# Second attention of a two-block model on one core: maximum inside the sum, another order of steps, outputs split in place

## The chip, the cores and the metric

One core of a Trainium2 chip runs the whole program. The time is device microseconds of one execution, and the number given is the median of the runs. The engines are PE (matmuls), DVE and ACT (vector and scalar work), POOL and SP (here the queue of the weight loads). Each has its own queue of instructions and executes it in order; engines meet in semaphores only.

## The reference, cut to what matters

Two model blocks follow each other on one sequence of 512 tokens of width 1024, in float32. The change touches the last layer of the second block alone, a differential attention with 8 heads of two score maps each:

```python
def diff_attention_layer(x, k, v, norm_g, w_in, lam_qk, sub_g, w_out, lambda_init):
    qg = rms_norm_2(x, norm_g) @ w_in
    q, gate = qg[..., :1024], qg[..., 1024:]        # q: 4 blocks of 128 tokens, 8 heads, 2 maps, 64
    lam = jnp.exp(jnp.sum(lf[0] * lf[1])) - jnp.exp(jnp.sum(lf[2] * lf[3])) + lambda_init
    slopes = 2.0 ** -jnp.arange(1, 9)
    def attend_block(args):
        scores = jnp.einsum("bhiqd,bhikd->bhiqk", qb, k) / math.sqrt(64)
        scores = scores - slopes[None, :, None, None, None] * dist
        probs = jax.nn.softmax(jnp.where(allowed, scores, -jnp.inf), axis=-1)
        weights = probs[:, :, 0] - lam * probs[:, :, 1]
        return jnp.einsum("bhqk,bhke->bqhe", weights, v)
    out = rms_norm_2(out, sub_g) * (1.0 - lambda_init)
    return x + (out * jax.nn.silu(gate)) @ w_out
```

`dist` is the distance of query and key, `allowed` holds for keys whose chunk of 64 is not later than the query's. A final RMS norm follows.

## The kernel before, in words

All matrices lie transposed in SBUF, eight tiles of 128 rows by 512 tokens. A dense product keeps float32 precision with three matmuls for each tile of 128 by 128: the weight and the activation are both split into a high part (type fp32r) and the rest (`xh`, `xl`; `wh`, `wl`), and high by high, high by low and low by high are added in PSUM (`product`, L387). A dense tile is so 8 x 3 = 24 matmuls of 512 columns.

Weights come in one long list of units (`weight_units`, L211), whose sequence is that of the program; the host packs them in that sequence. SP loads unit n into one of five buffers (L339), ACT writes the high half into one of three (`split_hi`, L351), DVE subtracts to get the low half (`split_lo`, L362). ACT and DVE work LA = 2 units ahead of PE, and wait for PE to be done with the unit three earlier.

The program has six stages: an S5 layer, a feed-forward, an attention, a feed-forward, a Mamba-2 layer and the second attention. Each engine walks through each stage with its own function (`att2_pe`, `att2_act`, `att2_dve`, `att2_pool`, from L2452). In the second attention all four walk over the same hand-made list of steps, `att2_order()` (L167), and each issues what its engine has in that step. The order of this list is therefore each engine's order of work.

The steps of the list, with the block number n = 4 x head + query block, or with the head or the tile m:

- `query m`, `gate m` (each one dense tile of `b_w_in_2`) and `out m` (tiles of `b_w_out_2`, first half: heads 0 to 3 only). ACT and DVE split the unit LA ahead in the same step. `queryB` (DVE, L2535) scales the query's result from PSUM, `gateB` multiplies the gate's with the norm (DVE, L2539) and takes its tanh (ACT, L2498), `gateC` finishes the gate (DVE, L2542), `outB` adds to h (L592).
- `scores n`: PE multiplies queries and keys of both maps (L2321), 128, 256, 384 or 512 key columns for query block 0 to 3, into four PSUM banks in turn.
- `exps n`: DVE adds the distances, times the slope, to each map (L2333), then reduces the maxima of both (L2337); ACT takes the exponential with the maximum as its bias and the sum as a second output (L2346).
- `combine n`: DVE inverts the sums, multiplies with lambda and forms the weights (L2355 to L2359).
- `turn n`: PE transposes the weights into one PSUM bank (L2367); `keep n`: ACT copies them out (L2375). The next `turn` needs that copy.
- `mix hd`: when the four blocks of a head are kept, PE multiplies them with the values (L2384). `sumsq hd`: ACT copies the result (L2393) and squares it (L2396), PE sums the squares over the head's 128 rows (L2402). `rs hd`: DVE forms the variance (L2408), ACT takes Ln and Exp for the inverse root (L2414, L2416; another table than the one of tanh). `tail hd`: DVE makes one Newton step in three instructions (L2422 to L2425), multiplies with the norm (L2428) and with the gate (L2431). `split hd`: DVE copies the high part into `xh` (L2437), POOL subtracts for the low part into `xl` (L2443).

The `xh` and `xl` tiles hold the attention's input until the last gate tile is done, so `split` waits for that (XUSED[10]), and the list places the splits there. After the list come the second halves of the eight output tiles, which need heads 4 to 7, then the sum of squares, the final norm (L2563) and the stores.

```python
        for r in list(running):
            out.append(r.pop(0))
        if 0 <= n - 4 < 32:
            out.append(("keep", n - 4))
            if (n - 4) % 4 == 3:
                running.append([("mix", hd), ("sumsq", hd), ("rs", hd), ("tail", hd)])
        if dense and n % 2 == 0:
            out.append(dense.pop(0))
```

In short (the full text is printed below), a slot n of the old list first takes one step of every running sequence, then `keep n-4`, `exps n-1`, `combine n-2`, `scores n`, every second slot a dense tile, and `turn n-3`. The first `out` comes in slot 31.

## Time and profile before

| what | value |
|---|---|
| runs, us | 2274.14, 2279.8, 2276.79; median 2276.79 |
| profiled execution, us | 2273.84 |
| its span, us | 2272.0 |
| granted TensorE clock over the span | 0.949 of full speed |
| second attention, from its first scores | 2012 us to the end |

The profiled execution's own time is 2273.84 us, 1.84 us more than its span; the span is what every view of the trace is counted in. Busy times of an engine are sums over its instructions; PE's are taken at the clock that was granted, so a slow stretch looks busier than a fast one. The idle time in front of an instruction is put down to what released it last.

### The profile page before, as it was taken

What the parts mean: (1) busy time and instruction counts of PE and PEld (TensorE: products, weight loads), DVE (VectorE), ACT (ScalarE), POOL (GpSimd) and SP (SyncE); (2) the same over time, 40 slices, a digit from 0 to 9 for tenths busy, and PEclk for the clock granted to TensorE, in tenths of its full rate; (3) what the DMA queues carried; (4) which work ended last, traced back from release to release, by engine and by line L of the source; (5) the groups of instructions that cost most, each with busy time, mean ns of one, the idle gap of its engine ahead of it and who ended that gap; (6) DMA issues with size and microseconds to landing.
All of it is one profiled execution on the core that took longest, in us unless ns stands there. A gap on an engine that the chain in (4) does not pass through costs nothing.

```text
span 2272.0 us, 24722 instructions
## 1 busy us (share of the span) xinstructions
PE 2036.6 (90%) x9332; PEld 1596.9 (70%) x9332; DVE 1450.1 (64%) x2058; ACT 829.2 (36%) x1246; POOL 227.1 (10%) x179
## 2 busy tenths in 40 slices
PE   5786899999999987799999998889999988998876
PEld 3575778888887855677888886667777767865545
DVE  7895457536644457647636645678787776257775
ACT  3334333222233335433322234344434334245542
POOL 2000010000010000010000010232222322000012
PEclk9887999999999989999999999899999999998888
DMA  5253423232232210022233222112222213321001
GB/s 194 71 132 81 133 74 103 83 111 95 81 112 94 83 57 1 1 85 93 83 111 97 84 91 83 46 52 65 70 64 66 71 46 100 108 67 42 19 28 60
DMA packets 86646, 178.32 MB, mean 78 GB/s; under 512 B 25856, under 2 KB 39296, under 8 KB 86528
## 3 DMA queue, kind: packets, MB, share of 16 engines
q1 hardware_dynamic: 84864, 171.56, 24.6%
q0 software_dynamic: 1376, 4.13, 0.6%
q8 instruction: 75, 1.23, 0.2%
q10 hardware_dynamic: 288, 1.05, 0.1%
q14 instruction: 43, 0.35, 0.0%
HBM read 169.43 MB, written 7.27 MB: 78 GB/s over the span
## 4 chain that ended last, share of the span: by engine, by line
PE 71%; DVE 15%; ACT 7%; issue 5%; DMA 1%; SPq 1%; POOL 0%; DVEq 0%; POOLq 0%; ACTq 0%
PE psum L398 18%; PE psum L401 17%; PE psum L399 17%; DVE wl L369 2%; PE psum L416 2%; PE psum L417 2%; PE psum L419 2%; ACT wh L358 1%; PE psum L761 1%; PE psum L763 1%; PE psum L762 1%; PE psum L1552 1%; PE psum L947 1%; PE psum L2384 1%; ACT ww L964 1%
## 5 line engine op out<-in xcount | busy, mean ns | idle before, releaser
L369 DVE TENSOR_TENSOR wl<-raw,wh 128x1024 fp32r<-128x1024 f32 (+3 forms) x337 | 385.4, 1144 | 433.4 <-ACT wh L358 432.9
L398 PE MATMUL psum<-xh,wh 128*128 128x512 f32 x1544 | 625.5, 405 | 20.9 <-DVE h L592 14.8
L401 PE MATMUL psum<-xh,wl 128*128 128x512 f32 x1544 | 610.3, 395 | 1.3 <-DVE wl L369 1.3
L399 PE MATMUL psum<-xl,wh 128*128 128x512 f32 x1544 | 609.8, 395 | 0.0
L358 ACT ACTIVATE wh<-raw 128x1024 fp32r<-128x1024 f32 (+3 forms) x337 | 314.9, 937 | 316.9 <-PE psum L401 214.3
L398 PEld LDWEIGHTS psum<-xh,wh 128*128 128x128 f32 x1544 | 295.6, 191 | 99.3 <-issue 17.5
L401 PEld LDWEIGHTS psum<-xh,wl 128*128 128x128 f32 x1544 | 294.9, 191 | 66.1 <-DVE wl L369 3.2
L399 PEld LDWEIGHTS psum<-xl,wh 128*128 128x128 f32 x1544 | 295.6, 191 | 65.0 <-issue 4.6
L515 POOL TENSOR_TENSOR rs<-rs,sq 128x512 f32<-128x512 f32 x49 | 67.1, 1369 | 1165.8 <-ACT sq L500 1164.9
L398 PE MATMUL psum<-fh,wh 128*128 128x512 f32 x352 | 139.2, 396 | 0.0
L401 PE MATMUL psum<-fh,wl 128*128 128x512 f32 x352 | 139.2, 396 | 0.0
L399 PE MATMUL psum<-fl,wh 128*128 128x512 f32 x352 | 139.2, 395 | 0.0
L592 DVE TENSOR_TENSOR h<-h,psum 128x512 f32<-128x512 f32 x88 | 60.2, 684 | 86.8 <-PE psum L401 85.7
L416 PE MATMUL psum<-xh,wh 128*128 128x512 f32 x184 | 77.3, 420 | 34.4 <-ACT wh L358 15.9
L401 PEld LDWEIGHTS psum<-fh,wl 128*128 128x128 f32 x352 | 66.1, 188 | 16.1
L399 PEld LDWEIGHTS psum<-fl,wh 128*128 128x128 f32 x352 | 66.1, 188 | 16.0
L398 PEld LDWEIGHTS psum<-fh,wh 128*128 128x128 f32 x352 | 66.1, 188 | 15.9
L419 PE MATMUL psum<-xh,wl 128*128 128x512 f32 x184 | 75.0, 408 | 1.4 <-DVE wl L369 1.4
L417 PE MATMUL psum<-xl,wh 128*128 128x512 f32 x184 | 75.1, 408 | 0.0
L480 ACT ACTIVATE xh<-h,par 128x512 fp32r<-128x512 f32 x64 | 44.0, 716 | 71.8 <-DVE h L592 56.6
L416 PEld LDWEIGHTS psum<-xh,wh 128*128 128x128 f32 x184 | 36.7, 200 | 45.3 <-issue 26.3
L398 PE MATMUL psum<-muh,wh 128*128 128x512 f32 x128 | 55.0, 429 | 8.7 <-POOL mul L1626 5.5
(430 smaller groups left out, 2994.4 us busy)
## 6 DMA issues: line engine op xcount, KB each, us to landing
raw<-d_w SPq DMA_DIRECT2D x224, 512.0 KB, 3.5
raw<-d_w SPq DMA_DIRECT2D x32, 384.0 KB, 3.0
raw<-d_w SPq DMA_DIRECT2D x48, 256.0 KB, 2.7
raw<-d_w SPq DMA_DIRECT2D x32, 320.0 KB, 2.9
Mt<-d_kd SPq DMA_DIRECT2D x64, 64.0 KB, 2.4
bc<-d_bc SPq DMA_DIRECT2D x8, 256.0 KB, 4.1
d_ud<-ust SPq DMA_DIRECT2D x8, 256.0 KB, 3.6
U<-d_ud SPq DMA_DIRECT2D x64, 32.0 KB, 2.1
```

Source lines behind the costliest of these rows:

```text
L358: act.e.activation(K.wh[n % NH][:, 0:COLS[n]], K.raw[n % RAW][:, 0:COLS[n]], ACT.Copy).then_inc(K.S["hi"], 1)
L369: dve.e.tensor_tensor(K.wl[n % NH][:, 0:COLS[n]], K.raw[n % RAW][:, 0:COLS[n]], K.wh[n % NH][:, 0:COLS[n]].bitcast(F32), ALU.subtract).the ...
L398: pe.e.matmul(b[:, :], WH[:, o:o + P], XH, start=(k == k0), stop=False)
L399: pe.e.matmul(b[:, :], WH[:, o:o + P], XL, start=False, stop=False)
L401: mm = pe.e.matmul(b[:, :], WL[:, o:o + P], XH, start=False, stop=(k == k1 - 1))
L416: pe.e.matmul(b[:, :], WH[:, o:o + P], XH, start=(k == 0), stop=False)
L417: pe.e.matmul(b[:, :], WH[:, o:o + P], XL, start=False, stop=False)
L419: mm = pe.e.matmul(b[:, :], WL[:, o:o + P], XH, start=False, stop=(k == 7))
L480: act.e.activation(K.xh[:, k, :], K.h[:, k, :], ACT.Copy, scale=K.par(gain, k)).then_inc(K.S["xh"], 1)
L515: pool.e.tensor_tensor(K.acc[:, :], K.acc[:, :], K.sq[k % 2][:, :], ALU.add).then_inc(K.S["acc"], 1)
L592: dve.e.tensor_tensor(K.h[:, m, :], K.h[:, m, :], K.bank[bank][:, :], ALU.add).then_inc(K.S[signal], 1)
L761: pe.e.matmul(b[:, :], XH[:, c], WH[:, kk * 512:(kk + 1) * 512], start=(k == 0), stop=False)
```

## The change

What it does, in the order of the diff:

- The list of steps is written anew. A slot n now holds, in this order: the steps put first (`queryB` and `gateB` one slot after their dense tile, `gateT` (the tanh, ACT) two after, `gateC` three after, `square` (the copy and the square of a mixed head, ACT), `outB`), `scores n`, a dense tile where one is due, `turn n-3`, `exps n-1`, `combine n-2`, `keep n-3`, and the steps put last. The 14 dense tiles stand in slots 0, 2, 5, 7, 10, 12, 14, 17, 19, 21, 24, 26, 29 and 31, the eight first output halves in slots 33 to 40. A head's end, from one slot after its fourth `keep`, takes one slot each for `mix`, `sumsq`, `rs`, `tailA` (the Newton step), `tailB` (the two products) and `split`, all as the slot's last steps, with `square` first in the slot of `sumsq`.
- Sum and maximum are one DVE instruction for each map. It adds scores and distances, multiplies by -2^-(hd+1), stores, and gives the minimum out into the bias. The query's scale holds 2^(hd+1) in return, and the exponential is taken with scale -1.
- The high part of a finished head goes by ACT into a tile `oh` of its own, the low part by POOL into `ol`. `oh` lies where the keys `kT2` lie and `ol` where the queries `qT2` lie, so the low part is written over the value it is made from; the high part waits until the head's scores are done (`asp`). The waits for the last gate tile are gone. The output product reads `oh` and `ol`.

```diff
--- before.py
+++ after.py
@@ -166,43 +166,42 @@
 def att2_order():
-    out = [("query", 0), ("queryB", 0), ("query", 1)]
-    running = [[("queryB", 1)]]
     dense = [x for m in range(8) for x in ([("query", m + 2)] if m < 6 else []) + [("gate", m)]]
-    outs, splits, n = list(range(8)), 0, 0
-    while n < 36 or running or splits < 8:
-        for r in list(running):
-            out.append(r.pop(0))
-            if not r:
-                running.remove(r)
-        if not dense and splits < 8 and ("tail", splits) in out:
-            out.append(("split", splits))
-            splits += 1
-        if 0 <= n - 4 < 32:
-            out.append(("keep", n - 4))
-            if (n - 4) % 4 == 3:
-                hd = (n - 4) // 4
-                running.append([("mix", hd), ("sumsq", hd), ("rs", hd), ("tail", hd)])
+    at = {(k * 31 + 6) // 13: x for k, x in enumerate(dense)}
+    assert len(at) == 14 and max(at) < 33
+    out = [("query", 0), ("queryB", 0), ("query", 1), ("queryB", 1)]
+    later = {}
+    for n in range(41):
+        out += later.get((n, "first"), [])
+        if n < 32:
+            out.append(("scores", n))
+        if n in at:
+            what, m = at[n]
+            out.append((what, m))
+            later.setdefault((n + 1, "first"), []).append((what + "B", m))
+            if what == "gate":
+                later.setdefault((n + 2, "first"), []).append(("gateT", m))
+                later.setdefault((n + 3, "first"), []).append(("gateC", m))
+        if 33 <= n:
+            out.append(("out", n - 33))
+            later.setdefault((n + 1, "first"), []).append(("outB", n - 33))
+        if 0 <= n - 3 < 32:
+            out.append(("turn", n - 3))
         if 0 <= n - 1 < 32:
             out.append(("exps", n - 1))
         if 0 <= n - 2 < 32:
             out.append(("combine", n - 2))
-        if n < 32:
-            out.append(("scores", n))
-        if dense and n % 2 == 0:
-            what, m = dense.pop(0)
-            out.append((what, m))
-            running.append([(what + c, m) for c in ("B", "C")] if what == "gate" else [(what + "B", m)])
-        if n >= 31 and outs:
-            m = outs.pop(0)
-            out.append(("out", m))
-            running.append([("outB", m)])
         if 0 <= n - 3 < 32:
-            out.append(("turn", n - 3))
-        n += 1
-    for m in outs:
-        out += [("out", m), ("outB", m)]
-    return out
+            out.append(("keep", n - 3))
+            if (n - 3) % 4 == 3:
+                hd = (n - 3) // 4
+                for k, what in enumerate(("mix", "sumsq", "rs", "tailA", "tailB", "split")):
+                    later.setdefault((n + 1 + k, "last"), []).append((what, hd))
+                later.setdefault((n + 2, "first"), []).append(("square", hd))
+        out += later.get((n, "last"), [])
+    return out + [("outB", 7)]
 S5_ORDER, MAMBA_ORDER, ATT2_ORDER = s5_order(), mamba_order(), att2_order()
@@ -2330,20 +2329,19 @@
     dve.wait_ge("ld", 16)
     for c in range(2):
         dve.wait_ge("asp", 2 * n + c + 1)
-        dve.e.scalar_tensor_tensor(out=S[:, c, 0:nk], in0=K.con("alibi")[:, T - nk:T], scalar=2.0 ** -(hd + 1),
-                                   in1=K.bank[2 + (2 * n + c) % 4][:, 0:nk], op0=ALU.mult, op1=ALU.add).then_inc(
-            K.S["asc"], 1)
-    dve.wait_ge("asc", 2 * n + 2)
-    dve.e.tensor_reduce(sv[:, 0:2], S[:, :, 0:nk], AX.X, ALU.max, negate=True).then_inc(K.S["amx"], 1)
+        last = dve.e.tensor_tensor_reduce(S[:, c, 0:nk], K.bank[2 + (2 * n + c) % 4][:, 0:nk],
+                                          K.con("alibi")[:, T - nk:T], -(2.0 ** -(hd + 1)), 3e38, ALU.add, ALU.min,
+                                          sv[:, c:c + 1])
+        last.then_inc(K.S["asc"], 1)
 def exps_act(K, act, n):
     nk = P * (n % 4 + 1)
     S, sv = K.Sb[n % 2], K.sml[:, n % 16, :]
-    act.wait_ge("amx", n + 1)
+    act.wait_ge("asc", 2 * n + 2)
     act.exp()
     for c in range(2):
-        act.e.activation(S[:, c, 0:nk], S[:, c, 0:nk], ACT.Exp, bias=sv[:, c:c + 1],
+        act.e.activation(S[:, c, 0:nk], S[:, c, 0:nk], ACT.Exp, scale=-1.0, bias=sv[:, c:c + 1],
                          accum_out=sv[:, 2 + c:3 + c]).then_inc(K.S["aex"], 1)
@@ -2416,14 +2414,19 @@
     act.e.activation(K.ny[:, :], K.ny[:, :], ACT.Exp, scale=-0.5).then_inc(K.S["any"], 1)
-def tail2_dve(K, dve, hd):
-    o, s, y, e = K.qT2[:, hd, :], K.ns, K.ny, dve.e
+def newton2_dve(K, dve, hd):
+    s, y, e = K.ns, K.ny, dve.e
     dve.wait_ge("any", hd + 1)
     own(K, dve, "dve", e.scalar_tensor_tensor(out=s[:, :], in0=y[:, :], scalar=-0.5, in1=y[:, :], op0=ALU.mult,
                                               op1=ALU.mult))
     own(K, dve, "dve", e.tensor_tensor(s[:, :], s[:, :], K.nv[:, :], ALU.mult))
-    own(K, dve, "dve", e.scalar_tensor_tensor(out=y[:, :], in0=s[:, :], scalar=1.5, in1=y[:, :], op0=ALU.add,
-                                              op1=ALU.mult))
+    e.scalar_tensor_tensor(out=y[:, :], in0=s[:, :], scalar=1.5, in1=y[:, :], op0=ALU.add,
+                           op1=ALU.mult).then_inc(K.S["dve"], dve.up())
+def tail2_dve(K, dve, hd):
+    o, y, e = K.qT2[:, hd, :], K.ny, dve.e
+    dve.wait_ge("dve", dve.n)
     dve.wait_ge("asq", hd + 1)
     own(K, dve, "dve", e.scalar_tensor_tensor(out=o, in0=o, scalar=K.lam[:, 6:7], in1=y[:, :], op0=ALU.mult,
                                               op1=ALU.mult))
@@ -2431,17 +2434,26 @@
     e.tensor_tensor(o, o, K.gS[hd % 4][:, :], ALU.mult).then_inc(K.S["aot"], 1)
-def split2_dve(K, dve, hd):
-    dve.wait_ge("aot", hd + 1)
-    dve.wait_ge("unit", XUSED[10])
-    dve.e.tensor_copy(K.xh[:, hd, :], K.qT2[:, hd, :]).then_inc(K.S["xh"], 1)
+def split2_act(K, act, hd):
+    act.wait_ge("aot", hd + 1)
+    act.wait_ge("asp", 8 * hd + 8)
+    act.e.activation(K.oh[:, hd, :], K.qT2[:, hd, :], ACT.Copy).then_inc(K.S["xh"], 1)
 def split2_pool(K, pool, hd):
     pool.wait_ge("xh", 88 + hd + 1)
-    pool.wait_ge("unit", XUSED[10])
-    pool.e.tensor_tensor(K.xl[:, hd, :], K.qT2[:, hd, :], K.xh[:, hd, :].bitcast(F32), ALU.subtract).then_inc(
+    pool.e.tensor_tensor(K.ol[:, hd, :], K.qT2[:, hd, :], K.oh[:, hd, :].bitcast(F32), ALU.subtract).then_inc(
         K.S["xl"], 1)
+def out2_x(K, pe):
+    def x(k):
+        pe.wait_ge("xh", 88 + k + 1)
+        pe.wait_ge("xl", 88 + k + 1)
+        return K.oh[:, k, :], K.ol[:, k, :]
+    return x
 def tile2(what, m):
@@ -2457,7 +2469,7 @@
     values_pe(K, pe, "w_kv_2", x, 8)
     x = x_of(K, pe, 10)
     product_pair(K, pe, "b_w_in_2", (0, 1), (0, 1), x, (("aqc", 1), ("aqc", 2)))
-    xo = x_of(K, pe, 11)
+    xo = out2_x(K, pe)
     for what, m in ATT2_ORDER:
         if what == "query" and m > 1:
             product(K, pe, "b_w_in_2", m, B2[(what, m)], x, ("aqc", m + 1))
@@ -2491,7 +2503,7 @@
     for what, m in ATT2_ORDER:
         if what in ("query", "gate", "out"):
             split_hi(K, act, done(*tile2(what, m)) + LA)
-        elif what == "gateB":
+        elif what == "gateT":
             act.wait_ge("agg", m + 1)
             act.wait_ge("agt", m - 1)
             act.other("tanh")
@@ -2500,8 +2512,10 @@
             keep2_act(K, act, m)
         elif what == "exps":
             exps_act(K, act, m)
-        elif what == "sumsq":
+        elif what == "square":
             sumsq_act(K, act, m)
+        elif what == "split":
+            split2_act(K, act, m)
         elif what == "rs":
             rs2_act(K, act, m)
     for m in range(8):
@@ -2532,7 +2546,7 @@
             split_lo(K, dve, done(*tile2(what, m)) + LA)
         elif what == "queryB":
             dve.wait_ge("unit", done(*tile2("query", m)))
-            dve.e.scalar_tensor_tensor(out=K.qT2[:, m, :], in0=K.bank[B2[("query", m)]][:, :], scalar=0.125,
+            dve.e.scalar_tensor_tensor(out=K.qT2[:, m, :], in0=K.bank[B2[("query", m)]][:, :], scalar=0.125 * 2.0 ** (m + 1),
                                        in1=K.rs[:, :], op0=ALU.mult, op1=ALU.mult).then_inc(K.S["aqc"], 1)
         elif what == "gateB":
             dve.wait_ge("aot", m - 3)
@@ -2549,10 +2563,10 @@
             combine2_dve(K, dve, m)
         elif what == "rs":
             rs2_dve(K, dve, m)
-        elif what == "tail":
+        elif what == "tailA":
+            newton2_dve(K, dve, m)
+        elif what == "tailB":
             tail2_dve(K, dve, m)
-        elif what == "split":
-            split2_dve(K, dve, m)
     for m in range(8):
         v = done("b_w_out_2", m, 4, 8)
         split_lo(K, dve, v + LA)
@@ -2736,9 +2750,13 @@
                     mamba_tensors(K, sb)
                 else:
                     att2_tensors(K, sb)
-                    K.kT2 = sb("k2T", [P, 8, T])
-                    K.qT2 = sb("q2T", [P, 8, T])
                     K.Vt["w_kv_2"] = sb("V2t", [P, 4, D])
+                    with ExitStack() as inner:
+                        sb = lambda name, shape, dt=F32: inner.enter_context(nc.sbuf_tensor(name, shape, dt))
+                        K.kT2, K.qT2 = sb("k2T", [P, 8, T]), sb("q2T", [P, 8, T])
+                    sb = lambda name, shape, dt=F32: part.enter_context(nc.sbuf_tensor(name, shape, dt))
+                    K.oh, K.ol = sb("oh", [P, 8, T], R32), sb("ol", [P, 8, T], R32)
         block = ctx.enter_context(nc.Block())
```

## Rows read from the trace of the kernel before

**Rows 1.** The page's first lines: span, and busy us, share, instructions of each engine
```profile
span 2272.0 us, 24722 instructions
...
PE 2036.6 (90%) x9332; PEld 1596.9 (70%) x9332; DVE 1450.1 (64%) x2058; ACT 829.2 (36%) x1246; POOL 227.1 (10%) x179
```

**Rows 2.** Busy time by stretch (count), granted clock, DMA share, GB/s
```profile
2012.00:2191.00 179.00, 147.70 (x595) 97.92 (x595) 135.88 (x282) 90.41 (x205) 5.14 (x4) 0.90 0.11 34
2191.00:2233.00 42.00, 34.05 (x137) 25.48 (x135) 30.70 (x54) 14.33 (x29) 5.78 (x4) 0.92 0.16 51
...
2255.00:2272.00 17.00, 2.07 (x2) 0.50 (x2) 8.79 (x13) 1.89 (x3) 1.75 (x2) 0.56 0.32 123
```

**Rows 3.** Same view, four heads of the loop: the first and the mean
```profile
2060.00:2086.00 26.00, 21.05 (x86) 14.15 (x85) 19.45 (x40) 13.56 (x29) 0.00 (x0) 0.87 0.13 41
...
sum 104.00, PE 83.75 PEld 56.17 DVE 77.28 ACT 54.30 POOL 0.00; mean PE 20.94 PEld 14.04 DVE 19.32 ACT 13.57 POOL 0.00
```

**Rows 4.** Waits, 2012 to 2233: engine, line, releaser, us in total, times, longest
```profile
ACT S L2346 <- DVE small L2337: 51.9, 24, 8.7
...
PE psum L2367 <- ACT wT L2375: 26.0, 8, 5.1
DVE wl L369 <- ACT wh L358: 22.5, 16, 2.6
```

**Rows 5.** Chain of waits, around one head's mix and at the end: start, us, what
```profile
2112.21 0.70 DVE nv L2408
2112.92 1.28 ACT L2685
2114.21 0.64 ACT ny L2414
...
2123.90 0.49 ACT wT L2375
...
2133.80 0.23 PE psum L398
...
2134.70 0.86 PE psum L2402 x2
...
2234.03 0.43 PE psum L399
```

**Rows 6.** Timeline of PE: start, us, engine, line, operation, idle before
```profile
2012.25 0.49 PE L2321 MATMUL psum<-k2T,q2T 64*128 64x128 f32 x4 [2.39 <-DVE q2T L2535]
...
2124.71 3.68 PE L2384 MATMUL psum<-wT,V2t 128*128 128x512 f32 x8
...
2190.99 0.50 PE L398 MATMUL psum<-xh,wh 128*128 128x512 f32 x1
...
2216.74 2.32 PE L2384 MATMUL psum<-wT,V2t 128*128 128x512 f32 x8
...
2233.27 0.77 PE L398 MATMUL psum<-xh,wh 128*128 128x512 f32 x1 [3.06 <-POOL xl L2443]
```

**Rows 7.** DVE groups by form, 2012 to 2255: count, busy us, mean ns, idle
```profile
L2333 DVE SCALAR_TENSOR_TENSOR S<-con,psum 128x512 f32<-128x512 f32 x16 | 10.2, 681 | 0.0
...
L2359 DVE SCALAR_TENSOR_TENSOR w<-S,small,w 128x512 f32<-128x512 f32 x8 | 6.0, 751 | 0.3
...
L2333 DVE SCALAR_TENSOR_TENSOR S<-con,psum 128x128 f32<-128x128 f32 x16 | 3.8, 279 | 0.0
...
L2359 DVE SCALAR_TENSOR_TENSOR w<-S,small,w 128x128 f32<-128x128 f32 x8 | 2.8, 351 | 0.3
```

**Rows 8.** Groups by line, 1900 to 2272
```profile
L2337 DVE TENSOR_REDUCE small<-S 128x2 f32<-128x256 f32 (+3 forms) x32 | 26.2, 820 | 1.1
...
L2346 ACT ACTIVATION_READ_ACCUMULATOR S<-S,small 128x1 f32 x64 | 12.0, 187 | 0.0
...
L2393 ACT ACTIVATE q2T<-psum 128x512 f32<-128x512 f32 x8 | 4.6, 577 | 1.5 <-PE psum L2384 1.5
L2437 DVE CAST xh<-q2T 128x512 fp32r<-128x512 f32 x8 | 3.4, 420 | 0.0
```

## The prediction

> **What bounds the kernel now.** The page's totals come first: PE is busy for 2036.6 of 2272.0 us, DVE for 1450.1 [rows 1]. That is an average over six stages, and the diff touches only the last, so the second view is the busy time by stretch. The loop over 32 score blocks runs from 2012 us to 2191 us, the eight first halves of the output product come among the last heads' work until about 2230, then the second halves until 2255, then the final norm and the stores (17 us) [rows 2]. In the first stretch PE is busy for 147.70 of 179 us and DVE for 135.88: neither is full. PE's figure is also flattered: the granted clock is 0.90, and four middle stretches of 26 us, one head each, repeat themselves with 20.9 us of PE, 19.3 of DVE and 13.6 of ACT in the mean, the first at a clock of 0.87 [rows 3]. Since no engine fills a head's 26 us, waits set the pace.
>
> The waits by engine say which [rows 4]. PE idles 26.0 us in 8 waits, up to 5.1 us each, for the copy of the turned weights (L2375); DVE idles 22.5 us for a high half of a weight (L358); ACT idles 51.9 us for the maxima (L2337). The chain of waits shows why these belong together [rows 5]. Once a head it runs in series: variance (L2408), a load of ACT's table 1.28, Ln, Exp, an earlier block's exponentials, a weight's high half, its low half on DVE, Newton steps, two products for the tail, the gate on DVE, its tanh, and only then the copy (0.49) that lets PE turn the next block and mix. From 2112.21 to 2124.4 PE is on none of it; it runs a dense product and the scores and then idles, and the mix behind takes 3.68 us at 2124.71, the same eight matmuls that take 2.32 at 2216.74 [rows 6]: the clock had fallen to the lower level after the idle stretch. The end has a second knot: at 2233.27 PE has waited 3.06 us for POOL's low half of head 7 [rows 6], and its following matmuls run 0.43 us apart where others of that form run 0.23 apart [rows 5].
>
> **The maximum in the sum.** 32 reductions (L2337) leave DVE, 820 ns each, 26.2 us [rows 8]. The 64 sums (L2333: 681 ns at 512 columns, 279 at 128 [rows 7]) become 64 instructions that add, scale, store and keep a minimum. The trace of before has none of that kind. Lower bound: nothing beyond the sum it replaces. Nearest row for a maximum or sum given out beside the stream: ACT's read of its accumulator, 187 ns [rows 8]; it overlaps the next exponential, and about half of it delays that one, so I take 0.10 us, 6.4 us in all. Upper bound: half the rate. Between 128 and 512 columns the sum rises by (681-279)/384 = 1.05 ns a column; 64 instructions over 20480 columns would then cost 21.4 us more.
> The two source streams and the reduced result invite one rule of the Trainium skill (Vector Engine (DVE) Microarchitecture Reference, "Points that are easy to get wrong"): a scalar-tensor-tensor with two sources in SBUF that are not bf16 halves its throughput, with no port left for the accumulator. The trace doesn't bear this out for f32: L2359 reads two SBUF tensors and takes 751 ns at 512 columns against 351 at 128, again 1.04 ns a column [rows 7]. [...]
> The scale of 2^(hd+1) goes into the query's factor and the sign into the exponential's scale: no instruction more, nothing. DVE so loses 26.2 - 6.4 = 19.8 us, of which what counts is about 2.5 us a head before the exponentials.
>
> **The splits of the outputs.** Eight casts of 420 ns leave DVE [rows 8]: 3.4 us. ACT gets eight copies of 128x512, 0.58 us by L2393 [rows 8]: 4.6 us on an engine that is busy 13.6 of 26. POOL's subtractions stay. The added wait for the scores of the head is met long before, since the head's mix follows them. Queued behind the ACT copy are the next exponentials; 0.6 us there is hidden by the slot of lag that DVE's combination has. Because results go to their own place, heads 0 to 6 are split as they come, none in a batch after the last gate.
>
> **The new order.** Both orders hold 14 dense tiles of 24 matmuls; the spacing goes from 2 slots (score blocks) to 31/13 = 2.38, so the first output half stands at slot 33, not 31. Table loads stay at 12 by the order of tanh and Ln. The gate is now three steps (product with rs, tanh, product), the norm's Newton steps and its last two products sit a slot apart, and each slot of DVE puts the maxima before the combination of the block ahead. SP loads the units in their new sequence; it runs up to five buffers ahead and DMA's share is 0.11 in the loop [rows 2], so nothing. No wait is on POOL before head 0's split.
>
> I walked four slots (one head) of the new lists by hand. Work: DVE 19.3 in rows 3, less 3.3 of reductions, plus 0.8, 16.8 us; PE, mix at full clock, about 18.0 with two dense tiles. What is left of waiting on DVE: some 1.1 us for a dense product to end before its result is taken, 0.9 for Ln and Exp behind the table load (1.28, 0.64, 0.64 [rows 5]), and 2 for a high half that stands behind a tanh and its load. Together 20.8 us, 5.2 a slot, where rows 3 have 6.5. No PE gap in it is over 2 us, so I leave the clock at its upper level. The first ten slots have four dense products (24 x 0.23 = 5.5 us each) but hardly norms or tails: the same walk gives 37.4 us. So the first output half starts 37.4 + 23 x 5.2 = 157 us after 2012.25, where it now starts 2190.99 - 2012.25 = 178.7 after [rows 6]: 21.7 less.
>
> **The end.** From the first output half to the second halves PE has 8 x 12 matmuls at 0.23, 22 us, mix 7 (2.1, by its 2.32 [rows 6] less the overlap with the next), two sums of squares (0.86 each [rows 5]) and two turns (0.8): 26.5 us. Now it takes 37.2 (2190.99 to about 2228.2, that is 2233.27 less 3.06 and less nine matmuls): 10.7 less. The tail of head 7 (rs, Ln, Exp, Newton, products, copy, low half) needs some 11 us and has outputs 3 to 7 before it, 13.7 us: the wait of 3.06 goes, and the eight matmuls at the lower clock behind it (8 x 0.2): 4.7 less. If that cover fails, these 4.7 come back. The second halves, the final norm and the stores (2255 to 2272 [rows 2]) stay.
> Sum: 21.7 + 10.7 + 4.7 = 37.1; I take off 1 for hand-overs that a walk doesn't count: 36. The profiled execution was 2273.84 (span 2272.0), 2.95 below the median of the runs, so this is 2237.8 for such an execution and 2241 against the median 2276.79. About 0.3% (7 us) is what a measurement here can tell from no change.
>
> **Rivals.**
> A. The new instruction runs at half rate, since its result needs a port beside the two streams: 21.4 us where I took 6.4, 15.0 more on DVE, plus what a later maximum costs ACT; DVE is then nearly full, so I count it whole: 2257. For it: a reduction and a two-source stream in one; against: L2359's slope. Chance 0.10. [...]
> B. The in-order queues keep a serial chain. ACT's copy of turned weights waits behind a dense product on PE, and Ln, Exp, tanh and the high half queue behind it; if this costs half of the 1.3 us a slot that I take away, 23 x 0.65 = 15 us return: 2256. For it: rows 5. Against: tail and gate no longer share a slot. Chance 0.13.
> C. The overlap is better and PE is the bound: 18.0 us a head where I have 20.8 gives 0.7 a slot, 16 us: 2225. For it: PE's work. Against: it allows no waiting. Chance 0.13.
> D. Slower. DVE has to change programs between its built-in operations and the added one, as ACT does with its tables (1.28 us, rows 5). Once a slot on DVE, the engine every slot passes: 32 x 1.28 = 41 us, 5 more than I gain: 2282. It decides from 36/32 = 1.1 us a slot. Against: no such change shows on DVE anywhere. Chance 0.03.
> My forecast keeps 0.61.
>
> **How the numbers follow.** 2241 is the likeliest. Its own spread is some 8 us; C reaches down to 2225, A and B to 2257 with their own spread. The range 2224 to 2260 leaves out most of D, and the outer parts of A, B and C, about 0.15. Faster by over 0.3%: all cases but D and a small part of B, 0.94; within 0.3%: 0.03; slower: 0.03.
>
> **What would show it.** No reduction, and 64 new instructions near 780 ns at 512 columns and 380 at 128; PE's wait for L2375 near a quarter of 26 us; a clock above 0.95 in the loop; score blocks 20.8 us a head; PE's first output half near 2169; no wait of PE for POOL at the end. A new instruction near 1.2 us at 512 columns means A; a wait of 3 us or more of PE once a head means B; DVE gaps before or behind each new pair mean D.

## The result and the profile after

The changed kernel takes **2252.02 us** (median of 4 runs, 2248.75 to 2258.05) where the kernel before takes 2278.3 (4 runs, 2274.14 to 2285.96): ratio 0.9884, interval 0.9849 to 0.9919, so 26 us less, 18 to 34 by the interval. A second measurement (e0 below) gave 0.9893 (0.9862 to 0.9924). The forecast was 36 less, 2241, with the range 2224 to 2260: direction and range hold, the size was 10 us too large.

First the totals of the page after, against [rows 1]:

```profile
span 2248.4 us, 24757 instructions
...
PE 2036.6 (91%) x9332; PEld 1596.5 (71%) x9332; DVE 1424.4 (63%) x2082; ACT 833.6 (37%) x1254; POOL 226.3 (10%) x179
```

Over the whole program PE's busy time is the same and the span 23.6 us less; DVE's busy time is 25.7 us less, ACT's 4.4 more. Where the gain lies is best read between five marks that both kernels have: the first scores, the scores of head 2's third block (slot 10), those of head 6's third block (slot 26), the first output half, and the last addition to h. The ten slots ahead of slot 10 are called the ramp below. Busy time by stretch, after; columns as in [rows 2]:

```profile
2016.00:2056.60 40.60, 38.45 (x162) 26.20 (x162) 24.65 (x78) 17.89 (x47) 0.00 (x0) 0.96 0.20 65
2056.60:2140.30 83.70, 75.79 (x313) 50.04 (x312) 64.90 (x170) 53.03 (x120) 4.71 (x4) 0.96 0.11 32
2140.30:2179.70 39.40, 33.40 (x133) 21.94 (x133) 27.43 (x71) 23.29 (x49) 1.69 (x2) 0.91 0.07 21
2179.70:2232.20 52.50, 50.55 (x211) 39.47 (x209) 34.41 (x55) 22.06 (x39) 11.52 (x9) 0.97 0.17 46
```

The same view of the kernel before, between the same marks:

```profile
2012.30:2058.80 46.50, 43.52 (x186) 30.60 (x186) 33.34 (x71) 19.53 (x50) 0.00 (x0) 0.96 0.19 61
2058.80:2162.90 104.10, 83.85 (x337) 56.23 (x336) 77.38 (x157) 54.22 (x118) 0.00 (x0) 0.89 0.10 29
2162.90:2191.00 28.10, 20.28 (x74) 11.04 (x73) 24.86 (x55) 16.66 (x39) 5.14 (x4) 0.82 0.03 10
2191.00:2255.00 64.00, 55.63 (x224) 42.95 (x222) 41.35 (x67) 21.36 (x41) 13.14 (x10) 0.92 0.12 38
```

The reader sees four things. The ramp is 6.1 us shorter, but it also holds one dense tile less (162 matmuls for 186, 5.1 us less of PE's work), because the new list spaces them more widely. Sixteen middle slots take 83.7 us instead of 104.1: PE is busy for 8.1 us less (24 matmuls fewer lie in it, and the clock is 0.96 instead of 0.89), and its idle time falls from 20.3 to 7.9. The last slots are 11.3 us *longer*, because 59 more matmuls, 13.1 us of PE's work, now lie in them and not ahead of them. The output products take 52.5 instead of 64.0, with 13 matmuls fewer in them, and PE is idle for 2.0 of them instead of 8.4. From the last addition to the end it is 16.2 against 17.05. Summed over these stretches PE's busy time falls by 6 us, the same matmuls at a higher granted clock, and its waiting by some 21. So from the first scores to the end the profiled executions take 232.3 against 259.8: 27.5 less. The first scores themselves stand at 2016.1 against 2012.25, 3.9 later, ahead of everything that was changed. Over all kernels of this study that mark lies anywhere from 2010.9 to 2024.6 us, with the same instructions in front of it. Therefore the experiments are compared by **the stretch from the first scores to the end**, and by medians where there are several runs. In e0 the stretch repeated as 232.3, though there the first scores stood in the same place too (2016.2). For another place only parts can be compared: in e7 the first scores stand 8 us later, and the ramp, the same list of steps there, takes 40.55 us against 40.50.

The waits after, 2012 to 2225, against [rows 4]:

```profile
ACT S L2344 <- DVE small L2332: 54.2, 22, 8.3
DVE wl L368 <- ACT wh L357: 43.2, 21, 5.5
...
PE psum L2400 <- ACT sq L2394: 6.1, 5, 2.7
...
PE psum L2365 <- ACT wT L2373: 5.9, 7, 1.7
```

PE's wait for the copy of turned weights fell from 26.0 us to 5.9. But DVE's wait for a weight's high half rose from 22.5 to 43.2, and the one for the squares, 8.6 us in 2 places before, is 6.1 in 5 (L2400). Each half of the change raises it by itself: it is 37.5 us in e1 below, which keeps the old order, and 36.1 (2020 to 2240) in e2, which keeps the old maximum. What the wait holds up is a matter of the order on DVE. Timeline of DVE in one head after (start, us, engine, line, operation, idle before):

```profile
2095.76 0.62 DVE L2357 SCALAR_TENSOR_TENSOR w<-S,small,w 128x384 f32<-128x384 f32 x1
2098.32 1.48 DVE L368 TENSOR_TENSOR wl<-raw,wh 128x1024 fp32r<-128x1024 f32 x1 [1.94 <-ACT wh L357]
2099.72 0.28 DVE L2332 CUSTOM_DVE_ANT_0 S<-psum,con 128x128 f32<-128x128 f32 x1
...
2106.49 0.69 DVE L2423 SCALAR_TENSOR_TENSOR ny<-xs,ny 128x512 f32<-128x512 f32 x1
2109.40 1.22 DVE L368 TENSOR_TENSOR wl<-raw,wh 128x1024 fp32r<-128x1024 f32 x1 [2.22 <-ACT wh L357]
2110.55 0.55 DVE L2332 CUSTOM_DVE_ANT_0 S<-psum,con 128x384 f32<-128x384 f32 x1
```

and ACT beside it:

```profile
2102.43 1.28 ACT L2699 ACT_TABLE_LOAD   x1
2103.72 0.63 ACT L2412 ACTIVATE ny<-nv 128x512 f32<-128x512 f32 x1
2104.38 0.63 ACT L2414 ACTIVATE ny<-ny 128x512 f32<-128x512 f32 x1
...
2105.90 0.58 ACT L2373 ACTIVATE wT<-psum 128x512 f32<-128x512 f32 x1
2106.50 1.28 ACT L2510 ACT_TABLE_LOAD   x1
2107.79 0.63 ACT L2510 ACTIVATE gt<-gate 128x512 f32<-128x512 f32 x1
2108.33 1.04 ACT L357 ACTIVATE wh<-raw 128x1024 fp32r<-128x1024 f32 x1
```

DVE stands 2.22 us for the high half (L357), which ACT makes only behind a table load and a tanh. Behind DVE's low half (L368) stand the maxima of the next block (L2332), whose scores PE has long finished and whose exponentials ACT needs next. Work that is due several slots later holds up work that is due now. The chain of waits of the kernel after goes round just that way:

```profile
2102.43 1.28 ACT L2699
2103.72 0.64 ACT ny L2412
...
2104.92 1.08 ACT S L2344 x4
2106.00 0.48 ACT wT L2373
2106.50 1.28 ACT L2510
2107.79 0.63 ACT gt L2510
2108.43 0.96 ACT wh L357
...
2109.40 0.04 DVE wl L368
...
2110.55 0.55 DVE S L2332
```

The new instruction, DVE's groups by form, 2016 to 2231, against [rows 7]:

```profile
L2332 DVE CUSTOM_DVE_ANT_0 S<-psum,con 128x512 f32<-128x512 f32 x16 | 10.4, 684 | 0.0
...
L2332 DVE DVE_READ_ACCUMULATOR2_ANT small<- 128x1 f32 x64 | 5.2, 82 | 0.0
...
L2332 DVE CUSTOM_DVE_ANT_0 S<-psum,con 128x128 f32<-128x128 f32 x16 | 3.9, 282 | 0.0
```

It takes 684 ns at 512 columns and 282 at 128, where the sum took 681 and 279: (684 - 282)/384 = 1.05 ns a column, the same slope. The result is handed out by a second instruction of 82 ns, which starts with the next one and lies beside it.

### The profile page after: what moved, and what is told of

Its sections match the earlier page's. It is cut to its first block, busy times and chain, and to the rows that moved or that the text cites. A ratio compares the mean times of both kernels' runs of the same rounds, so it can differ in the third digit from the quotient of the medians.

```text
span 2248.4 us, 24757 instructions
## 1 busy us (share of the span) xinstructions
PE 2036.6 (91%) x9332; PEld 1596.5 (71%) x9332; DVE 1424.4 (63%) x2082; ACT 833.6 (37%) x1254; POOL 226.3 (10%) x179
## 3 DMA queue, kind: packets, MB, share of 16 engines
q10 hardware_dynamic: 288, 1.05, 0.2%
## 4 chain that ended last, share of the span: by engine, by line
PE 70%; DVE 15%; ACT 7%; issue 5%; DMA 1%; SPq 1%; POOL 0%; DVEq 0%; POOLq 0%; ACTq 0%
PE psum L397 18%; PE psum L400 18%; PE psum L398 18%; PE psum L415 2%; PE psum L418 2%; PE psum L416 2%; DVE wl L368 2%; ACT wh L357 1%; PE psum L760 1%; PE psum L761 1%; PE psum L762 1%; PE psum L1551 1%; PE psum L946 1%; DVE S L2332 1%; ACT ww L963 1%
## 5 line engine op out<-in xcount | busy, mean ns | idle before, releaser
L368 DVE TENSOR_TENSOR wl<-raw,wh 128x1024 fp32r<-128x1024 f32 (+3 forms) x337 | 386.2, 1146 | 448.1 <-ACT wh L357 447.5
L397 PE MATMUL psum<-xh,wh 128*128 128x512 f32 x1480 | 596.8, 403 | 17.1 <-DVE h L591 14.9
L400 PE MATMUL psum<-xh,wl 128*128 128x512 f32 x1480 | 583.4, 394 | 1.3 <-DVE wl L368 1.3
L398 PE MATMUL psum<-xl,wh 128*128 128x512 f32 x1480 | 583.4, 394 | 0.0
L357 ACT ACTIVATE wh<-raw 128x1024 fp32r<-128x1024 f32 (+3 forms) x337 | 314.9, 937 | 320.6 <-PE psum L400 214.9
L397 PEld LDWEIGHTS psum<-xh,wh 128*128 128x128 f32 x1480 | 282.6, 191 | 93.3 <-DVE h L591 16.1
L400 PEld LDWEIGHTS psum<-xh,wl 128*128 128x128 f32 x1480 | 282.2, 191 | 63.4 <-DVE wl L368 3.2
L398 PEld LDWEIGHTS psum<-xl,wh 128*128 128x128 f32 x1480 | 282.5, 191 | 62.0 <-issue 3.9
L415 PE MATMUL psum<-xh,wh 128*128 128x512 f32 x184 | 79.9, 434 | 34.0 <-ACT wh L357 15.9
L418 PE MATMUL psum<-xh,wl 128*128 128x512 f32 x184 | 77.9, 424 | 2.5 <-DVE wl L368 2.5
L416 PE MATMUL psum<-xl,wh 128*128 128x512 f32 x184 | 77.5, 421 | 0.0
L400 PEld LDWEIGHTS psum<-fh,wl 128*128 128x128 f32 x352 | 66.0, 187 | 16.2
L415 PEld LDWEIGHTS psum<-xh,wh 128*128 128x128 f32 x184 | 38.3, 208 | 45.4 <-issue 26.0
```

What stands on the lines that cost most here:

```text
L357: act.e.activation(K.wh[n % NH][:, 0:COLS[n]], K.raw[n % RAW][:, 0:COLS[n]], ACT.Copy).then_inc(K.S["hi"], 1)
L368: dve.e.tensor_tensor(K.wl[n % NH][:, 0:COLS[n]], K.raw[n % RAW][:, 0:COLS[n]], K.wh[n % NH][:, 0:COLS[n]].bitcast(F32), ALU.subtract).the ...
L397: pe.e.matmul(b[:, :], WH[:, o:o + P], XH, start=(k == k0), stop=False)
L398: pe.e.matmul(b[:, :], WH[:, o:o + P], XL, start=False, stop=False)
L400: mm = pe.e.matmul(b[:, :], WL[:, o:o + P], XH, start=False, stop=(k == k1 - 1))
L415: pe.e.matmul(b[:, :], WH[:, o:o + P], XH, start=(k == 0), stop=False)
```

## The experiments

The theory ahead of them: the two halves of the change (maximum in the sum; order and splits) each bring part of the gain, and what is missing is lost on DVE's in-order queue behind the high half. The rivals: the maximum alone brings it all; the loss is in table loads, in the new instruction, or in PE itself.

**e1, the maximum alone**, in the kernel before:

```
-        dve.e.scalar_tensor_tensor(out=S[:, c, 0:nk], in0=K.con("alibi")[:, T - nk:T], scalar=2.0 ** -(hd + 1),
-                                   in1=K.bank[2 + (2 * n + c) % 4][:, 0:nk], op0=ALU.mult, op1=ALU.add).then_inc(
...
-    dve.e.tensor_reduce(sv[:, 0:2], S[:, :, 0:nk], AX.X, ALU.max, negate=True).then_inc(K.S["amx"], 1)
+        last = dve.e.tensor_tensor_reduce(S[:, c, 0:nk], K.bank[2 + (2 * n + c) % 4][:, 0:nk],
+                                          K.con("alibi")[:, T - nk:T], -(2.0 ** -(hd + 1)), 3e38, ALU.add, ALU.min,
+                                          sv[:, c:c + 1])
...
-            dve.e.scalar_tensor_tensor(out=K.qT2[:, m, :], in0=K.bank[B2[("query", m)]][:, :], scalar=0.125,
+            dve.e.scalar_tensor_tensor(out=K.qT2[:, m, :], in0=K.bank[B2[("query", m)]][:, :], scalar=0.125 * 2.0 ** (m + 1),
```

> The kernel before with the maximum taken in the sum alone; order and splits as before. Theory (the order carries the gain): the once-a-head chain of the old order (variance, table load, Ln, Exp, high half, low half, Newton, tail, gate, tanh, copy) holds no maximum, so the middle heads keep about 26 us each and only the slots at the start and at the end get shorter: 5 to 9 us less than before, ratio about 0.997. Rival (DVE's work carries the gain): 32 slots x 0.65 us = 21 us less, ratio about 0.991, and the middle heads at about 23 us. Both expect 64 new instructions as long as the sums they replace, and 64 reads of the accumulator of 82 ns.

Measured: 2263.29, ratio 0.9947 (0.9927 to 0.9967), 12 us less; the stretch is 246.4, 13.4 less. That is above the theory's 5 to 9 and below the rival's 21; the middle heads take 25.5 us, close to the theory's 26. The waits, 2012 to 2240:

```profile
DVE wl L369 <- ACT wh L358: 37.5, 22, 5.5
...
PE psum L2366 <- ACT wT L2374: 23.9, 7, 4.7
```

PE still waits 23.9 us for the turned weights: the old serial chain stays, and it is shorter only by what DVE spends less in it. A slot between 10 and 26 takes 6.38 us, before 6.51.

**e2, all but the maximum**: the changed kernel with the sum and the reduction of before (the diff of e1 turned round, in the new order).

> The changed kernel with the old sum and reduction; its order and its splits in place stay. Theory (the order carries the gain): 12 to 18 us less than before, ratio about 0.993, heads at about 22 to 23 us. Rival (DVE's work carries it): within 5 us of before.

Measured: 2261.32, ratio 0.9936 (0.9913 to 0.9959); the stretch is 246.7, 13.1 less (its profiled execution alone, 2273.15, would mislead: the first scores stand 12 us later in it than in before). That is within the expected 12 to 18; a middle head takes 23.5 us, a little over the expected 22 to 23. e1 and e2 add to 26.5 of the 27.5 us, but by stretch the parts aren't independent. In the old order the maximum takes 8.5 us off the time up to the first output half and 5.0 off the output halves (before against e1); in the new order it takes off 14.1 and 0.4 (e2 against after). In the slots the two help each other; in the output halves the new order leaves the maximum almost nothing to gain.

**e3, only the splits** in the kernel before: ACT makes the high halves of the outputs into a place of their own, as they come.

```
-                running.append([("mix", hd), ("sumsq", hd), ("rs", hd), ("tail", hd)])
+                running.append([("mix", hd), ("sumsq", hd), ("rs", hd), ("tail", hd), ("split", hd)])
...
-    dve.e.tensor_copy(K.xh[:, hd, :], K.qT2[:, hd, :]).then_inc(K.S["xh"], 1)
+    act.e.activation(K.oh[:, hd, :], K.qT2[:, hd, :], ACT.Copy).then_inc(K.S["xh"], 1)
```

> The kernel before with the splits of the finished heads in place, by ACT, one step after each head's tail; the old order otherwise, the old maximum. Theory: 3.4 us of copies leave DVE, but in the middle heads an ACT copy of 0.6 us is added to a chain that ACT is part of, and the wait of PE for head 7 at the end stays: within 4 us of before. Rival (the waits of the splits for the last gate tile cost time): 5 to 10 us less.

Measured: ratio 0.9982 (0.9965 to 0.9999), 2272.93; the stretch 255.1, 4.7 less, all of it at the end. That is just over the theory's 4 and under the rival's 5, and the interval of the runs holds both, but the slots keep their 6.51 us. At the end PE still waits:

```profile
2228.96 0.47 PE L395 MATMUL psum<-oh,wh 128*128 128x512 f32 x1 [2.37 <-POOL ol L2441]
```

So in e2 and after it is the new place of head 7's tail, not the split alone, that takes this wait away; and the rest of e2's gain, 13.1 less these 4.7, about 8 us if the parts add, is the order. Most of it shows in the output halves (58.9 in e3, 52.9 in e2), where the new order also has 13 matmuls fewer.

**e4, the low halves behind the maxima.** The weights' low half is taken after the block's combination; the rest is the changed kernel.

```
     for what, m in ATT2_ORDER:
-        if what in ("query", "gate", "out"):
+        if what == "out":
             split_lo(K, dve, done(*tile2(what, m)) + LA)
+        elif what in ("query", "gate"):
+            late = done(*tile2(what, m)) + LA
...
             combine2_dve(K, dve, m)
+            split_lo(K, dve, late)
```

> The changed kernel with DVE's low half of a query or gate weight made after the slot's combination of the weights instead of in front of its maxima. In the changed kernel DVE waits 24.6 us in 12 of these for ACT's high half, with the maxima and the combination queued behind. Theory (that in-order wait is what keeps a head at 20.3 us where PE's own work is 18): 6 to 12 us less than the changed kernel, about 2243 against its 2252, heads at 19 us. Rival (ACT's queue itself is late, the wait only shows it): within 3 us of the changed kernel.

Measured: 2244.88, ratio 0.985 (0.9826 to 0.9873); the stretch is 222.8, 9.5 less than after, within the expected 6 to 12. The medians differ by 7 to 9 us; the intervals of the two ratios overlap, so it is the stretch that carries this reading. No instruction was added or taken away. Busy time by stretch between the marks of above, from slot 10 on, and the waits, 2018 to 2231:

```profile
2062.41:2141.91 79.50, 73.85 (x314) 48.76 (x313) 66.42 (x170) 52.80 (x120) 5.08 (x4) 0.96 0.12 34
2141.91:2179.12 37.21, 32.23 (x134) 21.23 (x134) 29.30 (x78) 23.71 (x50) 1.66 (x2) 0.95 0.08 22
2179.12:2228.56 49.44, 48.92 (x211) 38.56 (x209) 32.74 (x49) 21.77 (x39) 11.87 (x9) 1.00 0.19 49
```

```profile
ACT S L2344 <- DVE small L2332: 26.2, 10, 8.3
DVE wl L368 <- ACT wh L357: 21.5, 11, 5.5
```

Both waits are half of the 54.2 and 43.2 of after, though only the order on DVE was changed: half of ACT's wait for the maxima went with DVE's wait for ACT. A slot takes 4.97 us between 10 and 26, after 5.23, so a head takes 19.9 where 19 was expected. The ramp is as long as after (40.55 us); the 9.5 us are 4.2 in the sixteen middle slots, 2.2 in the last ones and 3.1 in the output halves.

**e5, e4 and the sum of squares a slot later**, so that PE meets ready squares:

```
                 for k, what in enumerate(("mix", "sumsq", "rs", "tailA", "tailB", "split")):
+                    k += k > 0 and hd < 7
                     later.setdefault((n + 1 + k, "last"), []).append((what, hd))
```

> On top of e4_low_late: for heads 0 to 6 the sum of squares on PE and what follows it (rs, the two parts of the tail, the split) stand one slot later, so that ACT's copy and square after a mix have a slot of time. In the changed kernel PE waits 6.1 us in 5 waits at this sum, up to 2.7 us, and some matmuls behind run at the lower clock. Theory (PE's order is the next limit once DVE isn't held up): from the first scores to the end 222.8 us in e4_low_late become 214 to 219, heads below 19.5 us. Rival (the wait only moves to ACT, which is as late as before): 222 to 225.

Measured: 2235.71, ratio 0.981 (0.9781 to 0.9839); the stretch is 219.5, 3.3 less than e4, just above the expected 214 to 219 and below the rival's 222. No wait of PE for the squares is left. The slots from 10 on take 7.8 us less than in e4, but the ramp takes 1.9 more and the output halves 2.6 more, so the 3.3 us are the sum of both, not the price of the 6.1 us of waits alone.

**e6, no second table** (the tanh of the gates is left out: an exponential stands in its place, so ACT loads no table for it):

```
-            act.other("tanh")
-            act.e.activation(K.gt[m % 2][:, :], K.gS[m % 4][:, :], ACT.Tanh, scale=0.5)
+            act.e.activation(K.gt[m % 2][:, :], K.gS[m % 4][:, :], ACT.Exp, scale=0.5)
```

> The changed kernel with the tanh of the gates left out: an exponential stands in its place, so that ACT needs no other table in the loop. It leaves 12 table loads of 1.28 us, 15.4 us, away from ACT alone. Theory (the 24.6 us that DVE waits for high halves come from ACT's queue, where a load and a tanh stand ahead of the high half): from the first scores to the end 232.3 us become 222 to 227. Rival (ACT has slack, it is busy 13 of 20 us): 230 or more.

Measured, one run: 2236.51; the stretch is 219.2, 13.1 less than after, more than the expected 5 to 10. The page has 12 instructions less and 15.8 us less of ACT (833.6 to 817.8), that is 1.3 us for each load. Of ACT's saving 13.1 us came off the time. DVE's waits behind the loads are part of it:

```profile
ACT S L2344 <- DVE small L2332: 52.0, 23, 8.3
DVE wl L368 <- ACT wh L357: 33.6, 21, 5.5
```

DVE's wait for the high half falls by less than a quarter (43.2 to 33.6); the order of e4 is still the old one here.

**e7, the norm's two parts in one slot** (Newton steps and last products not a slot apart):

```
-                    later.setdefault((n + 1 + k, "last"), []).append((what, hd))
+                    later.setdefault((n + 1 + k - (k > 3), "last"), []).append((what, hd))
```

> The changed kernel with the Newton step and the two products of a head's tail in one slot again (the tail's second part and the split one slot earlier). Theory (small parts matter, since maxima and combination queue behind them): 1.4 us of DVE work move ahead of a slot's maxima; 232.3 us from the first scores to the end become 234 to 240. Rival (it is the place of the dense tiles and not this split that made the order faster): 231 to 234.

Measured, one run: 2263.39; the stretch is 237.4, 5.1 more than after, as expected. A slot takes 5.45 us. The split comes a slot earlier here too, so the 5 us are what the division of the norm and the place of the split are worth together.

**e8, the gate without its extra slot**: tanh and last product each one slot earlier.

```
-                later.setdefault((n + 2, "first"), []).append(("gateT", m))
-                later.setdefault((n + 3, "first"), []).append(("gateC", m))
+                later.setdefault((n + 1, "first"), []).append(("gateT", m))
+                later.setdefault((n + 2, "first"), []).append(("gateC", m))
```

> The changed kernel with a gate's tanh in the slot of its product with the norm and its last product one slot later, as the old order had them. Theory (the separate tanh keeps ACT from waiting for DVE's first work of a slot, with the exponentials behind it): 232.3 us from the first scores to the end become 236 to 244. Rival: within 2 us of it.

Measured, one run: 2257.65; the stretch is 232.3, the same as after to the tenth. The theory fails here and its rival holds: the slot that the gate was moved by serves nothing for the whole. It isn't without effect, though: the ramp is 0.9 us and the sixteen middle slots are 1.3 us longer, the last slots 0.6 and the output halves 1.6 shorter (granted clock 1.00 there, 0.97 after), and one profile can't say whether they would cancel again. In the forecast the new place of the gate had been part of what separates tail and gate.

**e9, one table for everything**, on top of e5. The gate's sigmoid is worked out with Exp, Ln and Exp, which are in the table that the norm uses anyway: exp(-ln(1 + exp(-x))).

```
-            act.other("tanh")
-            act.e.activation(K.gt[m % 2][:, :], K.gS[m % 4][:, :], ACT.Tanh, scale=0.5).then_inc(K.S["ag"], 1)
+            act.log_exp()
+            own(K, act, "act", act.e.activation(K.gt[m % 2][:, :], K.gS[m % 4][:, :], ACT.Exp, scale=-1.0))
+            own(K, act, "act", act.e.activation(K.gt[m % 2][:, :], K.gt[m % 2][:, :], ACT.Ln, bias=1.0))
+            act.e.activation(K.gt[m % 2][:, :], K.gt[m % 2][:, :], ACT.Exp, scale=-1.0).then_inc(K.S["ag"], 1)
...
-            dve.e.scalar_tensor_tensor(out=K.gS[m % 4][:, :], in0=K.gt[m % 2][:, :], scalar=1.0, in1=K.gS[m % 4][:, :],
-                                       op0=ALU.add, op1=ALU.mult).then_inc(K.S["agt"], 1)
+            dve.e.tensor_tensor(K.gS[m % 4][:, :], K.gt[m % 2][:, :], K.gS[m % 4][:, :], ALU.mult).then_inc(
+                K.S["agt"], 1)
```

> e5_sum_late with the gate's sigmoid from exp, ln(1 + x) and exp, which share a table with the loop's other functions: 8 times two more ACT instructions of 0.63 us (10.1 us) for 12 table loads of 1.28 us (15.4 us), and a product where the last step of the gate was. ACT's work falls by 5.3 us. Theory (ACT's queue is part of what is left, since leaving tanh and loads out gave 13 us in the changed kernel): from the first scores to the end 219.5 us become 212 to 217. Rival (after the two reorderings DVE and PE are the limit): 218 or more.

Measured: **2230.12**, ratio 0.9804 (0.9763 to 0.9846), 22 to 23 us less than the changed kernel's two medians (2252.02, 2253.51); the stretch is 215.2, within what was expected. The factor of one half that belongs to the tanh form goes out of the constant that scales the tail. This is the fastest kernel of the study. Busy time by stretch in its middle:

```profile
2060.00:2130.00 70.00, 68.01 (x300) 45.50 (x299) 60.79 (x158) 45.24 (x108) 3.85 (x3) 1.00 0.12 37
```

PE is busy for 68.01 of 70 us at the full clock: here PE is the bound that the forecast's rival C spoke of. Against e5 the last slots give 2.5 of the 4.3 us and the middle ones 1.8.

**e10, spacing of two slots**: dense tiles as near to each other as before the change (`at = {2 * k: x for k, x in enumerate(dense)}` for the spacing of 31/13), all else as changed.

> The changed kernel with a dense tile in every second slot again (the last in slot 26), all else in its new order. Theory (the spacing matters little for the sum, as PE's work is the same: the middle heads are slower, the last slots without dense tiles faster, and the first output halves wait no less): 230 to 236 us from the first scores to the end, where it is 232.3. Rival (the wider spacing is what breaks the chain): 240 or more.

Measured, one run: 2252.84; the stretch is 238.1, 5.8 more than after, between the theory's 230 to 236 and the rival's 240 and more. The wider spacing is thus worth 5.8 us: 9.1 up to the first output half, of which the output halves give 3.8 back (48.7 us here, 52.5 after), and 0.6 behind the last addition. The forecast had it as a mere statement of where the tiles stand. The run's time, 2252.84, hides this beside the profiled run of after, 2250.2, because its first scores stand at 2012.9 where after has 2016.1.

**e0, the changed kernel once more**, beside e9 and e10 on their chip.

> The changed kernel again, beside the versions below on the same chip. From the first scores to the end 232.3 us in the first profile. If this stretch repeats within 1 us while the start of the stretch moves by several, the scatter of the runs comes from the stages ahead of the change, and the stretch is the sharper measure of it.

Measured: 2253.51, ratio 0.9893 (0.9862 to 0.9924); stretch 232.3, as in the first profile. The other half of what was expected, a start that moves by several us while the stretch stays, didn't come up: the first scores stand at 2016.2, after 2016.1.

The profiled executions side by side, each from its first scores to its end, in us. What the two columns of parts leave of the stretch, 16 to 17 us, is the final norm and the stores. The first output half stands in slot 31 in before, e1 and e3 and in slot 33 in the others. The medians come from different measurements, in which the kernel before gave 2278.7 (e1 to e4), 2279.87 (e5 to e8) and 2275.01 (e9, e10).

| kernel | first scores | to the first output half | output halves | stretch | against before | median of runs |
|---|---|---|---|---|---|---|
| before | 2012.2 | 178.7 | 64.0 | 259.8 | | 2278.3 (n=4) |
| after | 2016.1 | 163.6 | 52.5 | 232.3 | -27.5 | 2252.02 (4) |
| e1 maximum alone | 2012.7 | 170.3 | 59.0 | 246.4 | -13.4 | 2263.29 (6) |
| e2 all but the maximum | 2024.6 | 177.7 | 52.9 | 246.7 | -13.1 | 2261.32 (5) |
| e3 splits alone | 2010.9 | 179.5 | 58.9 | 255.1 | -4.7 | 2272.93 (10) |
| e4 low halves late | 2021.9 | 157.3 | 49.4 | 222.8 | -37.0 | 2244.88 (4) |
| e5 and sums late | 2012.6 | 151.3 | 52.1 | 219.5 | -40.3 | 2235.71 (4) |
| e6 no tanh | 2015.5 | 154.3 | 48.8 | 219.2 | -40.6 | 2236.51 (1) |
| e7 norm in one slot | 2024.2 | 170.0 | 51.0 | 237.4 | -22.4 | 2263.39 (1) |
| e8 gate a slot earlier | 2023.5 | 165.2 | 50.9 | 232.3 | -27.5 | 2257.65 (1) |
| e9 one table | 2013.1 | 147.0 | 52.0 | 215.2 | -44.6 | 2230.12 (4) |
| e10 spacing of two | 2012.9 | 172.7 | 48.7 | 238.1 | -21.7 | 2252.84 (1) |

## Why the prediction was right in direction and too large in size

**What bounds the kernel**: right. Waits set the pace, not an engine; PE's work is the same and the time falls. The two knots named (the wait for L2375, the wait for POOL at the end) went as said: 26.0 to 5.9 us ("near a quarter"), and 3.06 to nothing.

**The term of the new instruction** was mis-sized. The forecast took 0.10 us for each over the sum, 6.4 in all, between 0 and 21.4. It measured 3 ns, at the lower bound: the read of the result (82 ns) lies beside the next instruction. The pair at 2093.69 and 2094.30 hands over to the reciprocal at 2094.91, after 1.22 us. **Rival A** (half rate) is out: 1.05 ns a column, where it wanted about 1.2 us at 512. The rule of the Trainium skill told beside it (Vector Engine (DVE) Microarchitecture Reference, "Points that are easy to get wrong") speaks of a scalar-tensor-tensor with both sources in SBUF. The new instruction takes one of its two from PSUM, so the rule didn't bear on it, and its 684 ns don't test it. What stands against the rule here is L2359 alone, which reads two SBUF tensors at 1.04 ns a column but keeps no sum. **Rival D** (changing programs on DVE) is out as well: the instruction follows others with no gap before or behind. This error made the forecast of the gain too small, not too large.

**The walk of the loop** was the step that failed, by its term for the start of the first output half, 157 us after the first scores in place of 178.7. It came to 163.6: 15.1 less and not 21.7. Split by the marks:

- The first ten slots: forecast 37.4, measured 40.5, 3.1 too little. PE alone is busy for 38.45 us there, more than the whole of the walk: it was PE's own work that was sized too small (four dense products at the full clock, where the clock is 0.96, which is 1.6 of the 40.6 us), and PE's 2.2 us of idle time come on top.
- The sixteen middle slots: forecast 5.2 each, 83.2; measured 83.7. That it came out so close is luck in part. The walked head had two dense tiles, eight in sixteen slots, where the new spacing puts seven there, 5.5 us of PE's work less; its 18.0 us of PE a head make 72 for eight tiles, where PE is busy for 75.79 with seven; and it left PE 11.2 us of idle time, where 7.9 are measured. Work sized too small and waiting sized too large made up for each other. Part of the work is clock, which stands at 0.96: some mixes still take 3.50 us (2087.95, behind a wait of 2.02) where others take 2.32 (2110.50), and the walk had the full clock.
- The last seven slots: forecast 36.4, measured 39.4, 3.0 too little, at a clock of 0.91. The walked head was taken for all, but slot 28 has 2.74 us for the squares of head 5 (L2400) in one piece, the longest wait of PE in the loop.

PE's waits in these last slots, timeline of PE:

```profile
2154.31 0.44 PE L2365 MATMUL psum<-con,w 128*128 128x128 f32 x2 [1.01 <-ACT wT L2373]
2157.49 2.04 PE L2400 MATMUL psum<-sq,con 128*128 128x512 f32 x2 [2.74 <-ACT sq L2394]
...
2179.21 1.10 PE L2400 MATMUL psum<-sq,con 128*128 128x512 f32 x2 [1.14 <-ACT sq L2394]
```

The two matmuls behind the wait of 2.74 take 2.04 us at a granted clock of 0.50 (2157.4 to 2159.5), where [rows 5] have 0.86 and the row at 2179.21 has 1.10: this wait cost more than its length. The forecast's "No PE gap in it is over 2 us" was wrong in two places (2.02 at 2085.73, 2.74 here), and its clock at the upper level in a third, where a wait of 1.67 at 2128.10 has a mix of 3.77 behind it, at a granted clock of 0.60.

**The end**: forecast 48.6 us from the first output half to the last addition (26.5, and the 22.1 of the second halves), measured 52.5. Two waits were not counted, and the matmuls behind them run slower at first:

```profile
2187.05 0.63 PE L2365 MATMUL psum<-con,w 128*128 128x128 f32 x4 [0.80 <-DVE w L2357]
2188.76 0.50 PE L397 MATMUL psum<-oh,wh 128*128 128x512 f32 x1 [1.08 <-DVE h L591]
2189.10 0.46 PE L398 MATMUL psum<-ol,wh 128*128 128x512 f32 x1
2189.35 0.63 PE L400 MATMUL psum<-oh,wl 128*128 128x512 f32 x1
```

That is 1.9 us of waits and, by the clock of 0.97 over 52.5 us, 1.6 of lower clock: 3.5 of the 3.9. Cover for head 7's tail held: no wait for POOL.

**The sum** by stretches: 15.1 and 11.5 and 0.9 (from the last addition to the end, where the forecast had nothing) make 27.5, against 21.7, 15.4 and none, less 1, that is 36.1.

**The cause** of what is missing is shown in part. In the ramp it is PE's work, sized too small, and no run takes it back: the ramp is 40.55 us in e4, 40.5 in e6, 42.4 in e5 and 42.5 in e9. In the last slots and the output halves it is waiting and the clock behind it, and moving the low halves (e4) takes back 2.2 of the 3.0 us and 3.1 of the 3.9. The 4.2 us that e4 takes off the middle slots were not missing there; they are part of the waiting that the forecast had seen ("2 for a high half that stands behind a tanh and its load") and had left in the time of a head. By the whole stretch the in-order wait of DVE for a high half ahead of the maxima is worth 9.5 us, the sum of squares a slot later 3.3 more, the second table 4.3 with both of these mended (13.1 by itself, e6).

**Rival B**, in-order queues that keep a serial chain, didn't come in the form told there, 15 us back through PE's turn and copy: PE waits 5.9 us for the copy. What came is its kin on DVE. The forecast's own sign of it, "a wait of 3 us or more of PE once a head", isn't met.

**Rival C** (PE is the bound) isn't true after, 75.79 of 83.70 us, but is in e9. What stays open: which piece of the 8 us between e3 and e2 belongs to which of the moved steps; e7 says 5.1 for the norm's division, e8 nothing for the gate's slot, e10 5.8 for the spacing, and these need not add. Whether the maximum in the sum gains by DVE's shorter work or by the exponentials' earlier start isn't told apart by e1. Kernels that move the table loads alone, with both tables kept, were not tried.

## What to carry to other kernels

Look on every in-order engine for work that is due late but waits for another engine, and put it behind what the next stage needs at once: here moving the low halves behind the combination cost no instruction and gave 9.5 us. Read a long wait "A for B" together with "B for A": here halving the one halved the other, so half of each was one ring. Judge parts of a change by stretch and not by their sum: e1 and e2 add up to the whole and still act on each other. And count the work that really lies in each stretch before a walk of one head is taken for all: the middle was right to 0.5 us by two errors that made up for each other, the two ends were off by 3 each.
